# Moving the issue of the experts' down weights from SyncE's DMA queue to ScalarE's own

## What is computed

```python
xb = xpad[idx_b]                                      # tokens of this expert
hb = jax.nn.silu(xb @ w_gate[e]) * (xb @ w_up[e])     # w_gate, w_up: 2048 x 512
return hb @ w_down[e]                                 # w_down: 512 x 2048
```

## Time and profile before

| | |
|---|---|
| median of 3 runs | 1729.98 us (1727.35 to 1730.0) |
| the profiled execution | 1730.94 us, of which the span from first to last instruction is 1729.0 us |
| mean granted clock of PE | 0.877 of full speed |
| busy: PE, DVE, ACT | 76%, 34%, 11% of the span |
| data moved | 486.95 MB |
| first wait for a piece that PE has in the experts' part | near 790 us |
| last matmul of expert 31's down weights | ends at 1719.14 us |

### The profile page before, as it was taken

How to read it: one execution, slowest core, us unless ns; L and a number is a source line. 1 busy time by engine, 2 the same in 40 slices (tenths; PEclk the granted TensorE clock), 3 DMA queues, 4 the chain that set the end, 5 groups by cost and what they waited for, 6 DMA issues and landing times.

```text
span 1729.0 us, 21665 instructions
## 1 busy us (share of the span) xinstructions
PE 1306.9 (76%) x8701; PEld 730.7 (42%) x8701; DVE 582.2 (34%) x901; ACT 193.2 (11%) x428; POOL 289.7 (17%) x378
## 2 busy tenths in 40 slices
PE   5999989899998999676675665656765755764857
PEld 4654545456666888562231322322322222321412
DVE  2199999992345100421120120220210301201314
ACT  3010101013222000200000000000000000000002
POOL 5966666661000200200000000000000000000000
PEclk9989989899999999888787898887877988868978
DMA  8331213133233993249999999999999999999995
GB/s 197 98 93 36 68 49 98 49 97 99 73 98 109 354 354 98 92 164 408 421 421 421 421 422 422 422 422 422 422 421 422 422 422 422 421 421 420 396 421 232
DMA packets 134732, 486.95 MB, mean 282 GB/s; under 512 B 20527, under 2 KB 83131, under 8 KB 83403
## 3 DMA queue, kind: packets, MB, share of 16 engines
q1 hardware_dynamic: 131776, 473.00, 69.7%
q0 software_dynamic: 2688, 12.97, 2.1%
q10 hardware_dynamic: 200, 0.02, 0.0%
HBM read 478.29 MB, written 10.78 MB: 283 GB/s over the span
## 4 chain that ended last, share of the span: by engine, by line
DMA 41%; PE 30%; DVE 4%; issue 2%; SPq 1%; ACT 1%; POOL 0%; POOLq 0%; DVEq 0%; ACTq 0%
DMA arena<-in_w_up 40%; PE ps L1856 6%; PE ps L1824 6%; PE ps L1994 6%; PE ps L1951 2%; PE ps L1860 2%; PE ps L1773 2%; DMA arena<-in_w_down 2%; PE ps L1901 1%; PE ps L2030 1%; SPq L515 1%; DVE arena L1508 1%; PE ps L1761 1%; PE ps L1722 0%; PE ps L1871 0%
## 5 line engine op out<-in xcount | busy, mean ns | idle before, releaser
L1994 PE MATMUL ps<-arena 128*32 128x256 f32 x4096 | 344.9, 492 | 240.8 <-DMA arena<-in_w_up 239.7
L1994 PEld LDWEIGHTS ps<-arena 128*32 128x32 f32 x4096 | 166.3, 135 | 437.6 <-issue 407.0
L1824 PE MATMUL ps<-arena 128*128 128x336 f32 (+1 forms) x1152 | 342.8, 455 | 0.0
L1824 PEld LDWEIGHTS ps<-arena 128*128 128x128 f32 x1152 | 221.3, 195 | 116.5 <-issue 26.7
L2030 PE MATMUL ps<-arena 128*32 128x512 f32 x1024 | 135.8, 645 | 59.7 <-DMA arena<-in_w_down 37.6
L606 POOL TENSOR_TENSOR arena<-arena 128x672 f32<-128x672 f32 (+5 forms) x148 | 138.9, 965 | 130.0 <-DVE arena L1205 112.1
L1525 DVE COPY arena<-ps 128x256 f32<-128x256 f32 x31 | 13.0, 420 | 424.8 <-PE ps L1994 424.8
L846 POOL DMA_INDIRECT arena<-hn_rows,arena x7 | 7.1, 1016 | 747.7 <-DVE arena L1528 710.1
L1856 PE MATMUL ps<-arena 128*128 128x256 f32 x512 | 112.6, 381 | 0.5 <-issue 0.5
L1508 DVE TENSOR_TENSOR arena<-arena,ps 128x1024 f32<-128x1024 f32 (+1 forms) x48 | 58.5, 1218 | 156.7 <-PE ps L1951 156.7
L1856 PEld LDWEIGHTS ps<-arena 128*128 128x128 f32 x512 | 96.8, 190 | 14.5 <-issue 1.9
(11 more groups left out here) (340 smaller groups left out, 1077.4 us busy)
## 6 DMA issues: line engine op xcount, KB each, us to landing
arena<-in_w_gate SPq DMA_DIRECT2D x128, 1024.0 KB, 23.6
arena<-in_w_up SPq DMA_DIRECT2D x128, 1024.0 KB, 25.7
arena<-in_w_down SPq DMA_DIRECT2D x128, 1024.0 KB, 26.2
arena<-in_w_in SPq DMA_DIRECT2D x16, 2048.0 KB, 8.9
arena<-in_w_out SPq DMA_DIRECT2D x8, 2048.0 KB, 10.2
arena<-in_state_gla SPq DMA_DIRECT2D x8, 512.0 KB, 9.1
arena<-in_w_glu SPq DMA_DIRECT2D x4, 1024.0 KB, 5.1
out_new_gla_sample<-arena SPq DMA_DIRECT2D x2, 2048.0 KB, 24.1
```

What stands on the lines that cost most here:

```text
L1824: mm = te.matmul(o, w, x, start=(k == 0), stop=(k == kt - 1))
L1994: mm = te.matmul(ps[CAP * x:CAP * x + CAP, 0, 256 * (i % 2):256 * (i % 2) + 256], xT[:, 4 * q + k, CAP * i:CAP * i + CAP], wpiece[2 * q + ...
```

## The change

ACT now issues d(n) for every expert but expert 0, on its own queue, at the head of its work for expert n; in program order that is after it copied its half of the outputs of expert n-1. The wait is for `weights_used` 12n, which ACT has already passed for that copy. SP issues g(n) alone. The waits ahead of g(n) are unchanged, and so are PE, DVE and POOL.

```diff
             with sp.Fori(1, NE - EPR) as e:
-                expert_weights(e, e, range(12))
+                expert_weights(e, e, range(8))
...
             for i in range(EPR):
-                expert_weights(NE - EPR + i, EPR * n_over + (NE - EPR + i), range(12))
+                expert_weights(NE - EPR + i, EPR * n_over + (NE - EPR + i), range(8))
...
-            def expert(m, i, inputs, last=False):
+            def down_weights(n, e):
+
+                act.wait_ge(weights_used, 12 * n)
+                for k in range(4):
+                    act.dma_start(wpiece[8 + k], A["w_down"][0][bass.ds(e, 1), 128 * k:128 * k + 128, :]
+                                  .rearrange("e p n -> (e p) n")).then_inc(piece_loaded[8 + k], 16)
+
+            def expert(m, i, inputs, last=False, e=None):
 
                 n = EPR * m + i
+                if not last and not (isinstance(n, int) and n == 0):
+                    down_weights(n, n if e is None else e)
                 if inputs is not None:
                     x_parts(inputs)
...
             m_last = n_over + (NROUND - 1)
-            expert(m_last, 0, m_last)
-            expert(m_last, 1, None)
-            expert(m_last, 2, None)
+            expert(m_last, 0, m_last, False, NE - EPR)
+            expert(m_last, 1, None, False, NE - EPR + 1)
+            expert(m_last, 2, None, False, NE - EPR + 2)
+            down_weights(EPR * m_last + (EPR - 1), NE - 1)
             load_table(ACT.Sqrt)
```

More of the change, by code:

```diff
@@ L538, in _ @@
                         e = sp.value_load(ovexp[0:1, bass.ds(EPR * o + i, 1)], min_val=0, max_val=NE - 1)
-                        expert_weights(e, EPR * o + (NE - EPR + i), range(12))
+                        expert_weights(e, EPR * o + (NE - EPR + i), range(8))
                 sp.nop()
             for i in range(EPR):
-                expert_weights(NE - EPR + i, EPR * n_over + (NE - EPR + i), range(12))
+                expert_weights(NE - EPR + i, EPR * n_over + (NE - EPR + i), range(8))
             outs = [A["y_prompt"][0, 0:128, :], A["y_prompt"][0, 128:256, :], A["y_sample"].rearrange("b t d -> (b t) d")]
@@ L1097, in _ @@
                 with act.If(n_over > o):
-                    expert(o + (NROUND - 1), 0, o + (NROUND - 1))
-                    for i in range(1, EPR):
-                        expert(o + (NROUND - 1), i, None)
+                    for i in range(EPR):
+                        e = act.value_load(ovexp[0:1, bass.ds(EPR * o + i, 1)], min_val=0, max_val=NE - 1)
+                        expert(o + (NROUND - 1), i, None if i else o + (NROUND - 1), False, e)
                 act.nop()
```

## The result

The changed kernel takes 1742.1 us (median of 14 runs, 1733.31 to 1750.0) against 1730.84 us before (14 runs). The ratio is 1.0059, 95% interval 1.0041 to 1.0076: 0.6% slower, some 10 us. The forecast was 1744 us.

A forecast was written before the change was run, and what follows sets the result against it. The prediction took one DMA stream of expert weights as the bound. It added 4 us (start), 3 (exit into round 7) and 7 (end) to 1730.94 for 1744.9, forecast as 1744 us, range 1731 to 1765.

The forecast's parts named there:

- The bound and the steady state: Experts' part: one DMA stream sets the pace, 29.84 us per expert; down waits move to quarters, no gain.
- Equal turns: While d(n) and g(n) are both in flight, each queue gets one half; d(n) needs 19.9 us.
- The one third of the earlier trace: POOL's fetch, 1257 to 1261 us: its queue held 33.7% of the engines' time, taken as a floor for d's share.
- Term 1: The start: d(1) waits for expert 0's output copies, so the stream has a hole; +4 us, bounds 3 and 5.5.
- Term 2: Exit into round 7: d(29) waits for expert 28, delayed by PE's standstill, leaving a hole; +3 us, bounds 0 and 6.
- ACT's own exit: ACT reads the overflow count before d(28): between nothing and PE's 9.51 us, at most 1.4 us more.
- Term 3: The end: last quarter starts at the stream's end, leaving 28.7 us behind it, not 21.7; +7 us, bounds 0 and 8.
- g(31) and d(31) run out nearly together: The end: 3.3 to 4.0 pieces of g(31) beside four of d(31), so the last quarter starts at the stream's end.
- The sum: Whole kernel: 1730.94 + 4 + 3 + 7 = 1744.9 us, forecast as 1744 us, 0.8% slower.
- The chain of down weights: Every expert: with a share below 0.38, d's loop exceeds 29.84 us and leaves holes; 1769 to 1848 us; chance 10%.
- d(31) last and no change: The end: d(31) still lands last, end term -3 us; 1731 to 1734, or 1727 to 1730 with holes covered; chance 12%.
- faster stream: Whole stream: a second queue keeps engines from pausing between pieces; 1% is 9 us, 2% is 18: 1726; chance 6%.

The follow-up runs named there:

- start and end together: The change, but SP issues d(1) and d(31) in its line again: 1734.97 us, ratio 1.0013 to the kernel before.
- act_plus4: The change, but ACT issues d(n) only after PE used two quarters of g(n), expert 28's input copies ahead: 1814.82 us, ratio 1.0467 to the kernel before.

## Why the prediction was right

**The bound and the steady state** held: 420 GB/s, no gain from shorter waits for down pieces (17.5 us for 37.6), which came back in the waits for quarters (290.6 us, forecast about 275). The forecast had them near zero after expert 1; 8 us of them are in expert 29. Two quarters, four pieces of the stream, start 9.97 us apart, so 2.49 us per piece stayed; the 0.8 MB that two lines lack in 770 us were not foreseen, and no loss of time by them is shown.

**Equal turns** held: 317 against 316 packets. The one third of the earlier trace rows was the floor it was taken for. The Trainium skill ("DMA: Bandwidth & Descriptors", Queues, rings and completion order) gives equal turns packet by packet, and the trace agrees.

**Term 1** was 4 us; the two windows give 3.6, the landings 2.7, giving d(1) back to SP 4.2 with some 4 us of uncertainty. The hole is there, though ACT issued 1.2 us earlier than counted.

**Term 2** was 3 us; the landings of the one profile give 3.6, giving it back measured 2.1, start and end together left 2.3. Neither time is significant alone, so the term is plausible and not shown. The profile shows it at 1642 to 1644 us, where the sum placed it: d(29) issued at 1641.7, with the line at its emptiest. ACT's own exit cost some 2.7 us (copies end at 1602.6, d(28) is issued at 1605.29), far less than the 9.51 us that bounded it.

**Term 3** was 7 us and was sized too high: giving d(31) back measured 5.2, with some 4 us of uncertainty, and the two profiles of the change show 0 and 3.1. Two steps made it too large. The first is "g(31) and d(31) run out nearly together": the last of g(31) landed 5.1 us ahead of the stream's end in the one profile and 1.0 in the other, and d(31) last gives part of the term back. The second is the 28.7 us behind the start of the last quarter. They were read from an execution whose next 16 down matmuls took 3.31 us; they took 1.92 us in both profiles of the change, and from the start of the last quarter to the end it was 26.8 and 25.8 us. With both put right the sum comes out: 26.8 - 4.9 - 21.9 = 0 us in the first profile and 25.8 - 0.9 - 21.9 = 3.0 us in the second, where 4.9 and 0.9 us lie between the start of the last quarter and the stream's end. The order may depend on when expert 30 ends, and so on its clock, as the two profiles suggest; and the wider scatter of the change (1733 to 1750 us against 1727 to 1737) may come from it. Neither was tested.

**The sum** was 14 us and came out as 10.2 us by the ratio (11.3 by the medians). That 1744 lies within 2 us of the median, 1742.1, is in part luck: the kernel before has its median at 1730.84 in these runs, where the three runs that I had gave 1729.98.

**The rivals.** The chain of down weights is real but was not near at the change's timing: it takes an issue two quarters later. I had put its edge by a sum that was some 3 us short from issue to landing (24.4 us for 21.7 in `act_plus4`), so it lies nearer than "some 6 us later" read; one quarter later it was not yet reached. d(31) last and no change: half of it happened in one profile (d(31) last by 5 us), while the holes were not covered. No faster stream was seen: 423 GB/s in two lines, as in one. No version ran that beats the kernel before; the one with the three places undone can't be told from it.

## What to carry to other kernels

When a stream of transfers is the bound, moving an issue costs what the engines lack at that moment: look for the places where the line is short (the first transfers, a stall of the consumer, the end), and sum them; in between, lateness is free (one quarter more cost nothing there) up to the point at which issue, transfer at its share and use make a loop longer than the period. A second queue adds no bandwidth, but it changes the order of arrival, which counts once, at the end, where the data with the longest work behind it should come first (some 5 us here by the times, with wide limits). And one profile of such an end is one draw: two executions of the same kernel differed there by 3 us, and kernels that all had one line at the end by 5, with PE's clock.

## What the runs showed of the hardware

ACT issued its transfers while its own copies ran: the first issue at 1298.65 us stands 0.14 us after the start of the first copy, though both copies come ahead of it in the program. And a load that meets an empty line is felt late: ACT's first issue of d(1) is at 788.54 us, the window from 788 to 790 moved only 49 GB/s, the ten microseconds after it 402.

The DMA engines drift apart in a long stream. In the kernel before, the first and the last of the 16 steps of a piece's semaphore are 2.7 us apart for the last up piece of expert 2, 4.9 at expert 6, 9.1 at expert 14 and 17.4 at expert 25. The spread grows in steps of about 2 us (the last of 4), one in each round of four experts, and is 7.0 us again at expert 29, behind the standstill. In the change it reached 19.4 us. Why it grows was not tested. At 2.487 us for a piece, 17.4 us are some 7 pieces (an estimate), so at the exit the fastest engines run dry that much ahead of the slowest, and a window there can lose bytes before the landings lose time.
